# Gate columns of the input projection computed beside the window K and V columns, by token

## The reference

```python
proj = x @ w_in[i]
(b_g, c_g, h, q, kc, vc, k_s, v_s, k_w, v_w, gates) = jnp.split(proj, split_points, axis=-1)
conv_out = b_g * _causal_dwconv(c_g * h, short_conv_w[i])
...
g = jax.nn.sigmoid(gates.astype(jnp.float32))
out = g[..., 0:1] * unchunk(o_c) + g[..., 1:2] * unchunk(o_s) + g[..., 2:3] * unchunk(o_w)
...
mixed = _head_rmsnorm(jnp.concatenate([conv_out, attn_out], -1), head_norm_g[i])
x = _layer_norm(ALPHA * x + mixed @ w_out[i], ln1_g[i], ln1_b[i])
u = _causal_dwconv(x @ w_up[i], ffn_conv_w[i]) + ffn_conv_b[i]
val, gate = u[..., :D_FF], u[..., D_FF:]
x = _layer_norm(ALPHA * x + (jax.nn.silu(gate) * val) @ w_down[i], ln2_g[i], ln2_b[i])
```

## Time and profile before

| | |
|---|---|
| median of 3 runs | 708.16 us (706.64 to 710.5) |
| profiled execution, its own time | 708.14 us |
| its span, first to last instruction | 706.2 us |
| PE busy | 689.5 us, 98% of the span |
| DVE busy | 519.5 us, 74% |
| ACT busy | 370.0 us, 52% |
| share of PE in the chain that ended last | 92% |
| mean clock granted to PE | 0.983 of full |

### The profile page before, as it was taken

One profiled execution on the slowest core, in us unless ns is written; L12 is line 12 of the kernel. 1 busy time (PEld: TensorE's weight loads), 2 busy tenths in 40 slices (PEclk: granted clock), 3 DMA queues, 4 the chain that ended last, 5 costly groups with the idle time before them and its releaser, 6 DMA issues.

```text
span 706.2 us, 11208 instructions
## 1 busy us (share of the span) xinstructions
PE 689.5 (98%) x4310; PEld 604.1 (86%) x4310; DVE 519.5 (74%) x762; ACT 370.0 (52%) x556; POOL 95.4 (14%) x54
## 2 busy tenths in 40 slices
PE   8999999999999999999999999999999999999995
PEld 5899998877998888888878999988889888888884
DVE  4675768768897777777696466697859977777756
ACT  5664535423776555666356443553248666666630
POOL 0000020221262111110000000204005511111000
PEclk9999999699999999999999999998999999999999
DMA  9971443332765555555338233513357855555301
GB/s 294 318 253 62 151 148 120 120 100 80 261 239 192 195 196 195 197 201 185 122 120 267 91 120 120 176 65 120 120 183 235 294 182 178 179 178 178 119 0 59
DMA packets 87401, 116.81 MB, mean 165 GB/s; under 512 B 5230, under 2 KB 73536, under 8 KB 87360
## 3 DMA queue, kind: packets, MB, share of 16 engines
q1 hardware_dynamic: 85920, 111.85, 47.6%
q10 hardware_dynamic: 1440, 4.39, 1.9%
HBM read 115.19 MB, written 1.05 MB: 165 GB/s over the span
## 4 chain that ended last, share of the span: by engine, by line
PE 92%; DVE 5%; DMA 1%; issue 1%; ACT 1%; SPq 0%; DVEq 0%; ACTq 0%
PE bank L1194 19%; PE bank L1196 18%; PE bank L1195 18%; PE bank L1454 17%; PE bank L1456 9%; PE bank L1279 3%; PE bank L1266 2%; DMA x_tok<-in_x 1%; PE bank L1215 1%; DVE x_tok L970 1%; DVE stats L954 1%; DVE x_tok L952 1%; PE bank L1258 1%; PE bank L1345 1%; DVE ring_lo L308 1%; DVE x_tok L978 1%
## 5 line engine op out<-in xcount | busy, mean ns | idle before, releaser
L308 DVE TENSOR_TENSOR ring_lo<-raw,ring_hi 128x2048 fp32r<-128x2048 f32 x102 | 232.6, 2285 | 23.0 <-ACT ring_hi L304 22.7
L304 ACT ACTIVATE ring_hi<-raw 128x2048 fp32r<-128x2048 f32 x102 | 194.3, 1908 | 13.2 <-DMA raw<-in_w_in 9.3
L1454 PE MATMUL bank<-xx,ring_hi 128*128 128x512 f32 x512 | 181.4, 398 | 0.0
L1456 PE MATMUL bank<-xx,ring_lo 128*128 128x256 f32 x512 | 143.8, 281 | 0.0
L1454 PEld LDWEIGHTS bank<-xx,ring_hi 128*128 128x128 f32 x512 | 96.2, 188 | 23.8
L1456 PEld LDWEIGHTS bank<-xx,ring_lo 128*128 128x128 f32 x512 | 96.7, 189 | 0.6
L721 POOL COPY step_par<-ffn_par 128x16 f32 (+1 forms) x22 | 64.3, 2927 | 221.5 <-DVE work L989 221.5
L1194 PE MATMUL bank<-xx,ring_hi 128*128 128x256 f32 x320 | 92.4, 289 | 0.0
L1195 PE MATMUL bank<-xx,ring_hi 128*128 128x256 f32 x320 | 90.5, 283 | 0.0
L1196 PE MATMUL bank<-xx,ring_lo 128*128 128x256 f32 x320 | 90.5, 283 | 0.0
L1194 PE MATMUL bank<-ring_hi,xx 128*128 128x512 f32 (+1 forms) x224 | 81.5, 364 | 3.8 <-DVE xx L783 3.8
(11 more groups left out here) (186 smaller groups left out, 998.1 us busy)
## 6 DMA issues: line engine op xcount, KB each, us to landing
raw<-in_w_up SPq DMA_DIRECT2D x44, 1024.0 KB, 5.2
raw<-in_w_down SPq DMA_DIRECT2D x22, 1024.0 KB, 5.0
raw<-in_w_in SPq DMA_DIRECT2D x21, 1024.0 KB, 5.2
raw<-in_cmp_w SPq DMA_DIRECT2D x8, 1024.0 KB, 5.9
raw<-in_w_out SPq DMA_DIRECT2D x8, 1024.0 KB, 4.8
qkv<-in_ln_g ACTq DMA_DIRECT2D x4, 512.0 KB, 3.6
qkv<-in_ln_b ACTq DMA_DIRECT2D x4, 512.0 KB, 5.0
raw<-in_w_in SPq DMA_DIRECT2D x2, 512.0 KB, 5.1
```

The source lines that it names most:

```text
L304: nc.scalar.activation(ring_hi[slot_of(L, u)][:], raw[raw_of(L, u)][:], ACT.Copy).then_inc(hi_done, 1)
L308: eng.tensor_tensor(ring_lo[slot_of(L, u)][:], raw[raw_of(L, u)][:], ring_hi[slot_of(L, u)][:].bitcast(fp32), ALU.subtract).then_inc(split ...
L1454: pe.matmul(dst[:], wh[:, k, P * c:P * (c + 1)], xx[:, k].rearrange("p a n -> p (a n)"), start=k == 0, stop=False)
L1456: ins = pe.matmul(dst[:, 0:SEQ], wl[:, k, P * c:P * (c + 1)], xh[:, k, :], start=False, stop=k == KT - 1)
```

## The change

The gate columns become columns 256 to 279 of unit 4. In the slots of the ring the unit is kept with 280 columns for each of the first seven input blocks (1960 of 2048 floats); the eighth block lies in a small buffer `kw_last`. ACT and DVE make the high and low parts of unit 4 in four pieces each (1792, 168, 256 and 24 elements per partition) instead of one of 2048 and one of 192 for the gates. PE issues the 48 matmuls of unit 4 with 280 moving columns; the 24 gate matmuls, the two transposes and PE's wait between them are gone, and so are the buffers `gate_wh`, `gate_wl` and `egateT`. The gates now come out with tokens on the partitions. ACT takes their exponential straight from bank 4 + t to `egate` ahead of the copy in `copy_kw`, 24 elements per partition and twice, and DVE adds 1 in place. `proj_done` counts three steps in a layer instead of four.

```diff
-        gate_wh = sb("gate_wh", [P, KT, NGATE], f32r)
-        gate_wl = sb("gate_wl", [P, KT, NGATE], f32r)
+        kw_last = sb("kw_last", [P, 2, 256 + NGATE], f32r)
...
+        def kw_pieces(L):
+
+            slot, src = slot_of(L, 4), raw[raw_of(L, 4)][:].rearrange("p (k n) -> p k n", k=KT)
+            halves = [r[slot][:, 0:(KT - 1) * (256 + NGATE)].rearrange("p (k n) -> p k n", k=KT - 1) for r in (ring_hi, ring_lo)]
+            return [([h[:, :, 0:256] for h in halves], src[:, 0:KT - 1, :]),
+                    ([h[:, :, 256:] for h in halves], gate_w[:, 0:KT - 1, :]),
+                    ([kw_last[:, a, 0:256] for a in range(2)], src[:, KT - 1, :]),
+                    ([kw_last[:, a, 256:] for a in range(2)], gate_w[:, KT - 1, :])]
...
+            def split_kw_hi(L):
+                act.wait_ge(raw_in[raw_of(L, 4)], 16 * (raw_round(L, 4) + 1))
+                act.wait_ge(slot_free[slot_of(L, 4)], CREDIT + slot_round(L, 4))
+                act.wait_ge(gate_in, 16 * (L + 1))
+                for (hi, _), src in kw_pieces(L):
+                    ins = nc.scalar.activation(hi, src, ACT.Copy)
+                ins.then_inc(hi_done, 1)
+
             def copy_kw(L, t):
...
+                nc.scalar.activation(egate[:, t, :], bank[4 + t][:, 256:256 + NGATE], ACT.Exp, scale=-1.0).then_inc(gates_in, 1)
                 nc.scalar.activation(kv_slots(t)[:, :, 2, :], bank[4 + t][:, 0:256].rearrange("p (b f) -> p b f", b=2),
                                      ACT.Copy).then_inc(qkv_copied, 1)
...
                 copy_q(L, 0)
-                act.wait_ge(gate_in, 16 * (L + 1))
-                nc.scalar.activation(gate_wh[:], gate_w[:], ACT.Copy).then_inc(gate_hi, 1)
...
                 copy_kw(L, 1)
-                act.wait_ge(proj_done, 4 * L + 4)
-                nc.scalar.activation(egateT[:], bank[7][0:NGATE, 0:SEQ], ACT.Exp, scale=-1.0).then_inc(gates_in, 1)
...
-                split_lo(V, L, 4)
-                dve.wait_ge(gate_hi, L + 1)
-                V.tensor_tensor(gate_wl[:], gate_w[:], gate_wh[:].bitcast(fp32), ALU.subtract).then_inc(gate_lo, 1)
+                dve.wait_ge(hi_done, L * NU + 5)
+                for (hi, lo), src in kw_pieces(L):
+                    ins = V.tensor_tensor(lo, src, hi.bitcast(fp32), ALU.subtract)
+                ins.then_inc(split_done[raw_of(L, 4)], 1)
...
-                dve.wait_ge(gates_T, L + 1)
-                chain.mark(V.tensor_scalar(egate[:].rearrange("p t n -> p (t n)"), bank[3][:, 448:448 + TT * NGATE], 1.0, None,
-                                           ALU.add))
+                dve.wait_ge(gates_in, 2 * L + 2)
+                gates = egate[:].rearrange("p t n -> p (t n)")
+                chain.mark(V.tensor_scalar(gates, gates, 1.0, None, ALU.add))
...
                     for k in range(KT):
-                        ins = mm3(bank[4 + t][:, 0:256], xh[:, k, tok], xl[:, k, tok], wh[:, k, :], wl[:, k, :], k == 0, k == KT - 1)
+                        hi, lo = (wh[:, k, :], wl[:, k, :]) if k < KT - 1 else (kw_last[:, 0, :], kw_last[:, 1, :])
+                        ins = mm3(bank[4 + t][:, 0:wide], xh[:, k, tok], xl[:, k, tok], hi, lo, k == 0, k == KT - 1)
...
-                pe.wait_ge(gate_lo, L + 1)
-                for k in range(KT):
-                    ins = mm3(bank[7][0:NGATE, 0:SEQ], gate_wh[:, k, :], gate_wl[:, k, :], xh[:, k, :], xl[:, k, :],
-                              k == 0, k == KT - 1)
-                ins.then_inc(proj_done, 1)
                 for part in range(2):
                     conv_unit(L, 0, part)
-
-                pe.wait_ge(gates_in, L + 1)
-                settled(pe)
-                for t in range(TT):
-                    ins = pe.transpose(bank[3][:, 448 + NGATE * t:448 + NGATE * (t + 1)], egateT[:, P * t:P * (t + 1)],
-                                       ident[0:NGATE, 0:NGATE])
-                ins.then_inc(gates_T, 1)
```

More of the change, by code:

```diff
@@ L182, in build @@
         b2 = sb("b2", [1, 2, HEAD])
-        egateT = sb("egateT", [NGATE, SEQ])
         egate = sb("egate", [P, TT, NGATE])
@@ L247, in build @@
         const_ready, masks_ready = sem("const_ready"), sem("masks_ready")
-        par_T, par_ready, gate_hi, gate_lo = sem("par_T"), sem("par_ready"), sem("gate_hi"), sem("gate_lo")
-        gates_in, gates_T = sem("gates_in"), sem("gates_T")
+        par_T, par_ready, gates_in = sem("par_T"), sem("par_ready"), sem("gates_in")
         x_ready, xT_done, xT_hi, xT_lo = sem("x_ready"), sem("xT_done"), sem("xT_hi"), [sem("xT_lo0"), sem("xT_lo1")]
@@ L433, in copy_q @@
                 if t == 0:
-                    act.wait_ge(proj_done, 4 * L + 1)
+                    act.wait_ge(proj_done, 3 * L + 1)
                 else:
@@ L446, in copy_kv @@
                 if t == 0:
-                    act.wait_ge(proj_done, 4 * L + 2)
+                    act.wait_ge(proj_done, 3 * L + 2)
                 else:
@@ L453, in copy_kv @@
                 ins.then_inc(qkv_copied, 1)
+            def split_kw_hi(L):
[5 more added lines that the diff above has]
+                ins.then_inc(hi_done, 1)
             def copy_kw(L, t):
                 if t == 0:
-                    act.wait_ge(proj_done, 4 * L + 3)
+                    act.wait_ge(proj_done, 3 * L + 3)
                 else:
                     unit_used(act, L, 4)
+                nc.scalar.activation(egate[:, t, :], bank[4 + t][:, 256:256 + NGATE], ACT.Exp, scale=-1.0).then_inc(gates_in, 1)
                 nc.scalar.activation(kv_slots(t)[:, :, 2, :], bank[4 + t][:, 0:256].rearrange("p (b f) -> p b f", b=2),
@@ L591, in _ @@
                     x_high(L, XT_BANK, 1, xT_done, xT_hi, (1,))
-                    for u in (2, 3, 4):
+                    for u in (2, 3):
                         split_hi(act, L, u)
+                    split_kw_hi(L)
                 else:
@@ L596, in _ @@
                     split_hi(act, L, 3)
-                    split_hi(act, L, 4)
+                    split_kw_hi(L)
                     x_high(L, XT_BANK, 1, xT_done, xT_hi)
                 copy_q(L, 0)
-                act.wait_ge(gate_in, 16 * (L + 1))
-                nc.scalar.activation(gate_wh[:], gate_w[:], ACT.Copy).then_inc(gate_hi, 1)
                 split_hi(act, L, 5)
@@ L1573, in _ @@
                 wait_unit(L, 4)
-                wh, wl = w_view(L, 4, KT)
+                wide = 256 + NGATE
+                wh, wl = (r[slot_of(L, 4)][:, 0:(KT - 1) * wide].rearrange("p (k n) -> p k n", k=KT - 1) for r in (ring_hi, ring_lo))
                 for t in range(TT):
```

## The result

The changed kernel takes 704.5 us (median of 22 runs, 699.4 to 712.8). The kernel before, run beside it on the same chip, takes 706.6 us (22 runs, 704.2 to 714.0). The ratio is 0.9948, with a 95% interval of 0.9927 to 0.997: 3.7 us saved, between 2.1 and 5.2. The medians by themselves lie 2.1 us apart and the means 3.5 us (704.0 against 707.5, with one slow run of the changed kernel, 712.8 us, left out). The forecast was 4.8 us, and 704.5 lies in its range. The direction is settled; the size is not settled to better than these 3 us.

A forecast was written before the change was run, and what follows sets the result against it. PE was taken to bound the kernel, busy in 98% of the span. Savings of 2.30 us in layer 0 and 2.51 in layer 1 took 708.14 to 703.3 us; forecast's own range 701.8 to 705.0, overall 700.2 to 706.8.

The forecast's parts named there:

- The gate products: PE, between unit 4 and the first convolution product: removing the 24 products saves 2.75 us in each layer.
- The transposes: PE, ahead of the query transposes: removing the gates' two saves 0.23 us in layer 0, 0.24 in layer 1.
- 24 columns more: PE, unit 4's 48 products: 280 moving columns instead of 256 cost 10.0 ns each, 0.48 us a layer.
- The high and low parts: Unit 4's four pieces: ACT 2.64 us against 2.27, DVE 2.94 against 2.64; unit 7's load up to 1.3 us later.
- The wait at the copy of half 0: PE, before layer 0's first convolution product: waits 0.2 us for ACT's copy, bounds 0 and 1.3 us.
- The table load in layer 1: ACT, ahead of the copy of half 0: the 1.28 us load costs nothing, with 1.9 us spare.
- The sum: Whole kernel: 2.30 us saved in layer 0 and 2.51 in layer 1, 708.14 - 4.8 = 703.3 us.
- the wait takes the place: Rival: copy of half 0 late by 1.3 us in layer 0, as much lost elsewhere; 705.3 us, chance 0.08.
- Given back later: Rival: a later stage of the layer is held by loads or DVE, its end unmoved; 708.1 us, chance 0.05.
- The clock falls otherwise: Rival: half-clock stretches at the attention's end change; worse 706.7 us, chance 0.10, better 699.9 us, chance 0.07.
- 280 at the price of 512: Rival: each of the 96 wide products costs 106.7 ns more, 10.2 us; 712.6 us, slower, chance 0.04.

The follow-up runs named there:

- filler: The changed kernel with 24 unused products put back in the gate products' old place in each layer; 708.1 us, ratio 1.0009.
- run without the joining: Against the kernel before: unit 4's weights split in four pieces, gates still computed by their own products and transposes; 706.14 us, ratio 0.9989.
- run with the copy first: The changed kernel with ACT's copy of half 0 ahead of unit 8's high split; 703.03 us, and 702.84 us when run again.
- ladder: The changed kernel plus unused products behind unit 4 in each layer, twelve each of eight widths from 30 to 512 moving columns; 734.73 us, one run.

## Why the prediction was right, and what it mis-sized

The forecast's mechanism holds: PE carries the chain, what leaves its list is time, and it comes back when the products are put back (filler, 708.1 us beside 707.8 of the kernel before; at equal clock +5.02 us, for 5.46 us of products less the 0.56 of the hole). The steps in the order of the prediction:

- **The gate products, 2.75 us a layer.** Right: with the other terms below, both layers close to within 0.05 us (layer 0: 2.75 - 0.49 - 0.62 + 0.37 = 2.01; layer 1: 2.75 - 0.44 + 0.38 = 2.69).
- **The transposes, 0.23 and 0.24.** Too small. I let the pause of 0.21 us ahead of a transpose stand. The query transposes start 0.12 us behind the last product: nearly the whole 0.44 is gone, 0.32, and their own first steps gained another 0.05. The forecast was 0.14 us too small in each layer. Whether the pause came from the gates' transposes themselves or from the wait ahead of them, no run tells.
- **24 columns more, 0.48 us a layer.** Right: 8.9 ns a product against 10.0, 0.49 and 0.44 us. The floor under 256 columns that I gave as the lower bound exists (112 ns), and 256 lies just above it.
- **The high and low parts.** Right to 0.05 us in each piece (ACT 1.71, 0.32, 0.40, 0.21; DVE 2.02 and 0.17 at its ends), a little too long in sum, since pieces overlap (ACT 2.36 us for 2.64, DVE 2.70 for 2.94). SP's load went out 1.45 us later, past the bound of 1.3; but only 0.85 of it come from the pieces, and 0.60 from the landing of unit 4's own load, which the forecast took as fixed.
- **The wait at the copy of half 0, 0.2 us.** This term was mis-sized. It was 0.56 us, and 0.06 more in the convolution part. I had put PE and the copy on the same instant by adding only the exponential, at 0.21 us. That moved the copy by 0.07 us (39.08 to 39.15); what moved it was unit 8's split, 0.56 us later (37.26 against 36.70). The sum had nothing for the late load of unit 7, and it came through on two ways. ACT split unit 7 late and was free 1.52 us later than before (37.19 against 35.67), which used up its idle 1.02 us ahead of unit 8's split and 0.5 more. And unit 8's load did not keep its time: it kept its issue (31.46 against 31.35) and landed 0.56 us late, beside unit 7's. The text named the second way ("unless unit 7's late transfer takes bandwidth from it") and gave the lateness a bound of 1.3 us, but put it at nothing in the sum. That the two loads shared the bandwidth is what the busier DMA engines suggest (1.08 against 0.87); no run moved one load alone. The run without the joining shows the lateness without the wait, the run with the copy first shows the wait gone.
- **The table load in layer 1.** Right: 1.28 us at 380.71, and no wait; the copy has 2.0 us to spare, where I had 1.9.
- **The sum.** The timelines give 4.71 us up to 421 us where 4.8 were forecast. Two errors of 0.4 us and 0.3 us cancelled: that it is so close is luck. And 704.5 lies as near to 703.3 as it does because the kernel before, run beside the changed one, had a median of 706.6 and not 708.16.

Of the rivals, *the wait takes the place* happened in part: 0.42 us beyond the forecast in layer 0, where it had 2.0. *Given back later* happened once, at L1313, for 0.35 us in the profiled pair (PE idled 0.5 to 0.8 us there in the traces of the changed kernel). The load behind it, issued 4.7 us earlier than before like all else, took 6.31 us to land instead of 5.04; why is open, for the DMA share over its flight was no higher (0.56 against 0.67). *The clock falls otherwise* is what made 4.4 us on the timeline into 2.7 in the profiled pair, and the mean clock over the runs, 0.003 lower, has up to 1.7 us of the gain's median by the slope. In the profiled pair 0.0019 of the 0.0044 is the end of the execution, which costs nothing, so some of the 1.7 us is not a cost of the clock. I had the clock as a case of its own with a chance, but it is rather a spread that lies on every case. *280 at the price of 512* is refuted by the kernel's own timeline and by the ladder.

Open: whether the lower mean clock of the changed kernel, as far as it costs time, is chance or comes from where its stretches lie in time; and 0.3 us that the gain has outside the span (time less span is 1.8 us in the kernels whose gates are not transposed, 2.1 in the two where they are).

## What to carry to other kernels

When an engine has work for 97% of the span, adding a few columns to a product that already has 256 is cheap (0.4 ns a column), and a separate product for few columns is not: 112 ns up to 128 moving columns, and 115 ns with 24 stationary and 256 moving ones. Put the copy that releases a bank ahead of the split that only feeds a later unit: when PE comes earlier, the order on the helping engine decides. Look at when a load lands and not only at when it goes out: here one that went out on time landed late, beside one that had gone out late. And compare differences of half a per cent at equal clock, or over many runs: here one kernel's runs lay up to 13 us apart while its timeline moved by tenths.

## What was not expected of the hardware

- At half clock, products of 128, 192 and 256 moving columns with 128x128 stationary all start 213 ns apart; at full clock it is 112 ns, measured up to 128 columns. So the floor of a product nearly doubles (1.9 times) when the clock is halved.
- The granted clock fell while PE was busy without a break: in the ladder during the products of 128 columns at 42.0 us, after 24 narrower ones at 112 ns each, and in every kernel at the attention's end. With wide products spread among the narrow ones, and 2.35 us more of waiting in each layer, the mean clock was 0.987 instead of 0.981.
- A single kernel's mean clock ranged from 0.967 to 0.992 between executions, and its span with it from 697.6 to 711.0 us.
- A load of the activation table took 1.28 us, and the exponential started 0.02 us behind it.
- A load whose issue moved by 0.1 us landed 0.56 us later, with the load ahead of it 1.5 us late.
